# Looked-up expert rows on GpSimd and VectorE: another schedule of the row groups and another first write of the gates

## The chip, the cores and the metric

The kernel runs on one core of one Trainium2 chip. The metric is the device time of one execution in microseconds. Three runs of the kernel before gave 4428.84, 4426.54 and 4429.15 us (median 4428.84).

## The reference, cut to what matters

One layer: a mixing stage (latent attention beside an RWKV scan), a cross attention, and a product-key expert layer ("PEER"), each added to the residual; 1024 tokens of width 1024, all in f32. The change touches the last of them alone:

```python
s = einsum('bshpd,hpkd->bshpk', q, sub_keys)         # 8 heads, 2 halves, 128 keys each
v1, i1 = top_k(s[..., 0, :], 16); v2, i2 = top_k(s[..., 1, :], 16)
cv, ci = top_k((v1[..., :, None] + v2[..., None, :]).reshape(..., 256), 16)
expert = e1 * 128 + e2                               # one of 16384, e1 and e2 by ci
gate = softmax(cv)
u = expert_u[it]; pre = einsum('tkd,td->tk', u, xt)  # it: 8 x 16 experts of a token
act = gelu(pre) * gate
out = einsum('tk,tkd->td', act, expert_v[it])
```

## The kernel before, in words

The stage `peer_stage` treats the 8 tiles of 128 tokens in two ways.

**Dense tiles.** Tiles 0 to 5 meet every expert. A first phase of 128 blocks (one block is 128 experts) computes gelu(u x) on TensorE (`block_in`, L1979) and stores it in `hidden_d`. Meanwhile VectorE picks the 16 experts of each (head, tile) unit (`choose`, in six pieces), and GpSimd scatters the unit's 16 columns of gates into `gates_d`, one indirect DMA per column (L1960), adding to zeros that an earlier stage wrote. Then two output passes multiply hidden value and gate and sum over experts (`block_out`, L2070): pass 0 for tiles 0 to 3, 128 blocks; pass 1 for tiles 4 and 5, again 128 blocks. Each output block loads 512 KB of expert rows and two pieces of `hidden_d` and `gates_d`.

**Looked-up tiles.** Tiles 6 and 7 fetch their experts instead: 2 tiles x 8 heads x 16 = 256 look-ups, each an indirect DMA on GpSimd's queue (`look_up`, L1940) of one 8 KB row (u beside v) for each of 128 tokens, 1 MB. VectorE works on them in groups of two: `row_hidden` (L2348) takes the dot product with u, ScalarE the gelu, `row_sums` (L2360, L2363) adds gate x v to the sum. After `row_sums` the buffer is given back (`row_used`).

**What sets the order.** Every engine walks by hand-written slots: WT = 16 slots of the query projection, then slots 16 to 143 (the first phase), then 144 to 271 (pass 0) and 272 to 399 (pass 1). `unit_pieces` says in which slots a unit is chosen: one unit per slot up to slot 14, then one unit in three slots. `group_slot` says in which slot a group's dot products stand, `sums_at` in which its sums. The first EARLY_SLOTS look-ups use a ring of 8 buffers, all later ones a ring of 6 (`RING_IN`, `RING_OUT`): look-up p waits until row p - 8, or p - 6, was given back.

GpSimd's queue holds scatters and look-ups in one line. `rows_by` spreads EARLY_SLOTS look-ups evenly over the 384 scatters of dense units 7 to 30, and PASS_SLOTS over the 256 scatters of units 32 to 47; the rest follows behind the last scatter. The first look-up of the second ring waits for the end of the first phase. Pass 1 may load gates only when all scatters have landed. A waiting look-up holds up all scatters behind it.

Of the kernel before, what the change touches and what calls it, by code (L numbers as in the profile page):

```python
# [10 lines left out]
ALU = mybir.AluOpType  # L11
# [22 lines left out]
NK = 128  # L34
# [1617 lines left out]

DENSE = NT - 2
PASSES = ((0, 1, 2, 3), (4, 5))
EARLY_SLOTS, PASS_SLOTS = 148, 64
RING_IN, RING_OUT = 8, 6
TD = DENSE * P
HD = TD // 2
# [4 lines left out]
GROUP = 2  # L1663
HOME_ROWS = 4
WT = 2 * PH
FIRST_UNIT = 4


def unit_order():
# [6 lines left out]
def unit_pieces():  # L1676


    at, slot = {}, FIRST_UNIT
    for n in range(UNITS):  # L1680
# [9 lines left out]
def peer_stage(nc, consts, h, high, low, rstd, w_query, keys_d, expert_u, expert_uv, fin_row, scores_d, hidden_d, gates_d, h_d,  # L1690
# [10 lines left out]
    OUT = WT + NK  # L1701
    with Stage(nc, "peer") as st:
# [15 lines left out]
        idx, gates = st.sb("idx", [P, UNITS, TOPK], U32), st.sb("gates", [P, UNITS, TOPK])  # L1718
# [31 lines left out]
        added = [st.sem(f"added{i}") for i in range(4)]  # L1750
# [43 lines left out]
        def group_slot(g):  # L1794

            if g < EARLY_SLOTS // GROUP:
                return WT + 14 + (g * 29) // 20
            g -= EARLY_SLOTS // GROUP
            if g < PASS_SLOTS // GROUP:
                return OUT + 4 + (g * 17) // 5  # L1800
            return OUT + NK + 2 + 5 * (g - PASS_SLOTS // GROUP)

        groups = SLOTS // GROUP
        groups_at = {group_slot(g): g for g in range(groups)}
        gelu_at = {group_slot(g) + 2: g for g in range(groups)}
        lasts = (EARLY_SLOTS // GROUP - 1, groups - 1)
        sums_at = {group_slot(g) + 4 if g in lasts else group_slot(g + 1) + 2: g for g in range(groups)}
        assert len(groups_at) == len(gelu_at) == len(sums_at) == groups
        row_end = max(sums_at) + 1

# [18 lines left out]
        def _(sp):  # L1829
# [8 lines left out]
            def load_raw(b):  # L1838
                if b >= 3:
                    sp.wait_ge(u_low, b - 2)  # L1840
                sp.dma_start(raw[b % 3][:, :], w_query[b] if b < WT else expert_u[b - WT]).then_inc(raw_ready[b % 3], 16)
# [34 lines left out]
            for b in range(WT):  # L1876
                load_raw(b + 3)
                if b >= 2:
                    store_scores(b - 2)
                if b == FIRST_UNIT - 1:  # L1880
                    load_scores(0)
                    load_scores(1)
                next_scores(b)
# [37 lines left out]
        @block.gpsimd  # L1921
        def _(pool):
            def look_up(p):
                n, k = row_place(p)[1:]
                buffer, ready, use = rows(p)
                pool.wait_ge(idx_ready, n + 1)
                if p == 0:
                    pool.wait_ge(h_stored, 16)
                    pool.wait_ge(rows_full, 2 * SPARSE)
                    pool.wait_ge(scaled, 2 * KC)  # L1930
                    pool.wait_ge(s_mm, WT)
                    for i in range(2):
                        pool.wait_ge(w_stored[i], 16 * PH)
                if p < EARLY_SLOTS and p >= RING_IN:
                    pool.wait_ge(row_used, p - RING_IN + 1)
                if p == EARLY_SLOTS:
                    pool.wait_ge(mm_done, WT + NK)
                if p >= EARLY_SLOTS + RING_OUT:
                    pool.wait_ge(row_used, p - RING_OUT + 1)
                pool.indirect_dma_start(buffer[:, :], None, expert_uv,  # L1940
                                        bass.IndirectOffsetOnAxis(ap=idx[:, n, k:k + 1], axis=0)).then_inc(ready, 16)

            def add_squares():
                for m in range(KC // 2):
                    pool.wait_ge(sq_ready, 2 * m + 2)
                    if m >= 2:
                        pool.wait_ge(sq_summed, m - 1)
                    nc.gpsimd.tensor_tensor(sq_sum[:, m % 2, :], sq[:, 0, :], sq[:, 1, :], ALU.add).then_inc(sq_added, 1)

            nc.gpsimd.iota(iota_i[:, :], [[1, TOPK]], base=0, channel_multiplier=0).then_inc(iota_ready, 1)  # L1950
            nc.gpsimd.iota(tok_i[:, :], [[P, NT]], base=0, channel_multiplier=1).then_inc(iota_ready, 1)
            add_squares()
            turn = 0
            for i, n in enumerate(dense):
                head, tile = units[n]
                pool.wait_ge(idx_ready, n + 1)
                if scatters(head - 1, tile):
                    pool.wait_ge(added[tile % 4], scatters(head - 1, tile))
                for k in range(TOPK):
                    pool.indirect_dma_start(gates_flat, bass.IndirectOffsetOnAxis(ap=idx[:, n, k:k + 1], axis=0),  # L1960
                                            gates[:, n, k:k + 1], None, compute_op=ALU.add).then_inc(added[tile % 4], 16)
                    for p in range(turn, rows_by(i, k)):
                        look_up(p)
                    turn = max(turn, rows_by(i, k))
            for p in range(turn, SLOTS):
                look_up(p)
            for tile in range(4):
                pool.wait_ge(added[tile], scatters(PH - 1, tile + 4 if tile + 4 < DENSE else tile))
# [630 lines left out]
```

## Time and profile before

| | us |
|---|---|
| median of 3 runs | 4428.84 |
| profiled execution, its own time | 4427.99 |
| its span in the trace | 4426.4 |
| first phase, first block_in matmul to last | about 1891 to 3116 |
| pass 0, output blocks | about 3144 to 3930 |
| pass 1, to the last matmul | about 3938 to 4416 |

Times in the trace count from the start of the span. The share of an engine over the whole span says little here, since the three phases have different limits; the tables by stretch are to be read, and in them the busy time of each engine beside the stretch's length. GpSimd's busy time leaves out some 0.30 us ahead of each of its DMAs, which the profile calls issue; the two together are what one DMA costs that queue.

### The profile page before, as it was taken

To read this page: it belongs to the slowest core of one execution; us is meant where nothing else is said; L and a number is where in the kernel's file an instruction comes from. 1 tells how busy PE (TensorE), PEld (TensorE's weight loads), DVE (VectorE), ACT (ScalarE), POOL (GpSimd) and SP (SyncE) were. 2 spreads that over 40 slices of the span, in tenths; PEclk is the share of its full clock that TensorE was granted. 3 is DMA by queue.
4 is the path that set the end of the run, shared out by engine and by line. 5 is a ranking of instruction groups with operands and counts; after the bars stand their busy time and mean duration, and the time that the engine had idled before them with its cause. 6 is when DMAs were issued, how large, how long until landed. Compare 5 with 4: busy or idle time off the path is not lost.

```text
span 4426.4 us, 54973 instructions
## 1 busy us (share of the span) xinstructions
PE 3834.4 (87%) x19168; PEld 3258.1 (74%) x19168; DVE 2790.5 (63%) x5235; ACT 1263.5 (29%) x1846; POOL 2019.4 (46%) x1384
## 2 busy tenths in 40 slices
PE   7958788888888889999889888989789999988878
PEld 5834377787766567899889888889667777876666
DVE  5453367677313336847777777767798666557776
ACT  2113323332102212233232222222333222233334
POOL 1023132424000001888878888887567888301110
PEclk9979889898889999999999999999999999998899
DMA  2249200000221023548788878876778899869886
GB/s 100 95 158 400 107 17 8 17 8 8 72 90 38 0 71 105 93 92 265 235 254 244 243 235 244 249 246 185 249 235 269 271 281 290 283 215 307 306 308 230
DMA packets 376334, 788.59 MB, mean 178 GB/s; under 512 B 137104, under 2 KB 211856, under 8 KB 342288
## 3 DMA queue, kind: packets, MB, share of 16 engines
q1 hardware_dynamic: 210320, 451.28, 30.4%
q0 software_dynamic: 165888, 336.01, 26.0%
q8 instruction: 33, 0.54, 0.1%
q14 instruction: 93, 0.76, 0.0%
HBM read 643.09 MB, written 144.05 MB: 178 GB/s over the span
## 4 chain that ended last, share of the span: by engine, by line
PE 14%; DMA 13%; DVE 12%; POOL 9%; issue 8%; DVEq 3%; ACT 2%; SPq 1%; POOLq 0%; ACTq 0%
POOL gates_d L1960 7%; PE peer_ps L2070 5%; PE peer_ps L1979 5%; DVE peer_acc L2363 4%; PE peer_ps L1993 4%; DMA late_in<-gates_d 3%; DMA peer_rows<-in_expert_uv,peer_idx 3%; DMA late_rows<-in_expert_uv,peer_idx 3%; DMA rows<-in_expert_uv,peer_idx 2%; DMA peer_gat<-gates_d 1%; DVEq L2278 1%; DVEq L2362 1%; POOL peer_rows L1940 1%; DVE late_in L2370 1%; DVE peer_rows L2348 1%
## 5 line engine op out<-in xcount | busy, mean ns | idle before, releaser
L1960 POOL DMA_INDIRECT gates_d<-peer_gates,peer_idx x768 | 1353.3, 1762 | 320.9 <-issue 219.7
L1979 PE MATMUL peer_ps<-high,peer_uh 128*128 128x384 f32 x2048 | 540.4, 345 | 116.3 <-DVE peer_ul L2265 105.5
L1979 PE MATMUL peer_ps<-low,peer_uh 128*128 128x384 f32 x2048 | 533.5, 342 | 0.0
L1979 PE MATMUL peer_ps<-high,peer_ul 128*128 128x384 f32 x2048 | 531.7, 341 | 0.0
L1979 PEld LDWEIGHTS peer_ps<-high,peer_uh 128*128 128x128 f32 x2048 | 377.8, 194 | 133.1 <-issue 107.4
L2070 PE MATMUL peer_ps<-peer_vh,peer_ah 128*128 128x512 f32 x1028 | 339.5, 413 | 103.7 <-DVE peer_al L2382 103.6
L1940 POOL DMA_INDIRECT late_rows<-in_expert_uv,peer_idx x108 | 140.1, 1297 | 562.9 <-DVE peer_acc L2363 497.0
L2116 ACT ACTIVATE peer_uh<-peer_raw 128x1024 fp32r<-128x1024 f32 x144 | 152.4, 1058 | 813.5 <-PE peer_ps L1979 698.9
L1979 PEld LDWEIGHTS peer_ps<-low,peer_uh 128*128 128x128 f32 x2048 | 382.0, 194 | 0.0
L1979 PEld LDWEIGHTS peer_ps<-high,peer_ul 128*128 128x128 f32 x2048 | 381.2, 193 | 0.0
L2070 PE MATMUL peer_ps<-peer_vh,peer_al 128*128 128x512 f32 x1028 | 331.5, 405 | 0.0
L2070 PE MATMUL peer_ps<-peer_vl,peer_ah 128*128 128x512 f32 x1028 | 329.5, 403 | 0.0
L2070 PEld LDWEIGHTS peer_ps<-peer_vh,peer_ah 128*128 128x128 f32 x1028 | 199.8, 199 | 162.8 <-DVE peer_al L2382 121.6
L2265 DVE TENSOR_TENSOR peer_ul<-peer_raw,peer_uh 128x1024 fp32r<-128x1024 f32 x144 | 177.2, 1231 | 96.4 <-ACT peer_uh L2116 87.3
L2070 PEld LDWEIGHTS peer_ps<-peer_vh,peer_al 128*128 128x128 f32 x1028 | 202.9, 197 | 45.4
L2070 PEld LDWEIGHTS peer_ps<-peer_vl,peer_ah 128*128 128x128 f32 x1028 | 201.7, 196 | 44.9
L2348 DVE CUSTOM_DVE_ANT_0 late_rows<-late_rows,peer_xrow 128x1024 f32<-128x1024 f32 x108 | 129.5, 1221 | 138.5 <-DMA late_rows<-in_expert_uv,peer_idx 138.5
L2070 PE MATMUL peer_ps<-peer_uh,peer_ah 128*128 128x512 f32 x508 | 169.1, 415 | 53.5 <-DVE peer_al L2382 53.5
L2164 ACT ACTIVATE peer_ah<-late_in 128x512 fp32r<-128x512 f32 (+1 forms) x170 | 88.2, 519 | 285.5 <-DVE late_in L2370 268.9
L2070 PE MATMUL peer_ps<-peer_uh,peer_al 128*128 128x512 f32 x508 | 166.0, 409 | 0.0
L2070 PE MATMUL peer_ps<-peer_ul,peer_ah 128*128 128x512 f32 x508 | 165.7, 408 | 0.0
L2070 PEld LDWEIGHTS peer_ps<-peer_uh,peer_ah 128*128 128x128 f32 x508 | 98.6, 198 | 83.7 <-DVE peer_al L2382 61.7
(437 smaller groups left out, 7858.0 us busy)
## 6 DMA issues: line engine op xcount, KB each, us to landing
late_in<-in_expert_uv SPq DMA_DIRECT2D x170, 512.0 KB
gates_d<-mla_zeros POOLq DMA_DIRECT2D x128, 512.0 KB
peer_raw<-in_expert_u SPq DMA_DIRECT2D x128, 512.0 KB
hidden_d<-peer_hid SPq DMA_DIRECT2D x128, 384.0 KB
peer_val<-in_expert_uv SPq DMA_DIRECT2D x86, 512.0 KB
late_in<-hidden_d SPq DMA_DIRECT2D x85, 256.0 KB
late_in<-gates_d SPq DMA_DIRECT2D x85, 256.0 KB
gates_d<-peer_gates,peer_idx POOLq DMA_INDIRECT x768
```

The costliest lines, as they stand in the source:

```text
L1940: pool.indirect_dma_start(buffer[:, :], None, expert_uv, bass.IndirectOffsetOnAxis(ap=idx[:, n, k:k + 1], axis=0)).then_inc(ready, 16)
L1960: pool.indirect_dma_start(gates_flat, bass.IndirectOffsetOnAxis(ap=idx[:, n, k:k + 1], axis=0), gates[:, n, k:k + 1], None, compute_op=ALU ...
L1979: last = nc.tensor.matmul(ps[i][:, a, 0:HD], w[:, cols], x[:, kc, a * HD:(a + 1) * HD], start=(kc == 0 and w is uh[i % 2] and x is high), ...
L1993: last = nc.tensor.matmul(ps[i][:, a, :], w[:, cols], x[:, kc, a * HALF:(a + 1) * HALF], start=(kc == 0 and w is uh[i] and x is high), sto ...
L2070: last = nc.tensor.matmul(ps[i][:, a, :], x[:, i * P:(i + 1) * P], w[:, a * HALF:(a + 1) * HALF], start=(first_block and x is ah[r] and w ...
L2116: nc.scalar.activation(uh[b % 2][:, :], raw[b % 3][:, :], ACT.Copy).then_inc(u_high, 1)
L2164: nc.scalar.activation(ah[q % RING][:, 0:n], act_in[q % 3][:, 0:n], ACT.Copy).then_inc(a_high, 1)
L2265: nc.vector.tensor_tensor(ul[b % 2][:, :], raw[b % 3][:, :], uh[b % 2][:, :].bitcast(F32), ALU.subtract).then_inc(u_low, 1)
L2278: dve.drain()
L2348: nc.vector.tensor_tensor_reduce(out=buffer[:, 0:D], in0=buffer[:, 0:D], in1=xrow[row_place(p)[0]][:, :], scale=1.0, scalar=0.0, op0=ALU.m ...
L2362: dve.drain()
L2363: nc.vector.scalar_tensor_tensor(out=acc[tile][:, :], in0=rows(p)[0][:, D:2 * D], scalar=pre[:, p:p + 1], in1=acc[tile][:, :], op0=ALU.mul ...
```

## The change

Five edits in one file:

- EARLY_SLOTS and PASS_SLOTS go from 148, 64 (44 left) to 144, 72 (40 left): four look-ups fewer in the first phase, eight more in pass 0, four fewer behind it.
- Early groups stand 4 slots later (WT + 18 instead of WT + 14, the same 29/20 slots between them). Groups of pass 0 stand every 3 slots from OUT + 7, instead of every 3.4 from OUT + 4. Those of pass 1 keep their slots, but there are two groups fewer.
- The sums of all groups from the last early one on follow 3 slots behind the dot products. Before, they stood 2 slots behind the next group's dot products.
- FIRST_UNIT is 3, not 4: the first unit is chosen one slot sooner, 12 instead of 11 units fit in ahead of the first phase, and all later units move three slots forward. The load of the first scores stays where it was.
- For head 0 the scatter writes the gates (`bypass`) and does not add them.

```diff
-EARLY_SLOTS, PASS_SLOTS = 148, 64
+EARLY_SLOTS, PASS_SLOTS = 144, 72
-FIRST_UNIT = 4
+FIRST_UNIT = 3
             if g < EARLY_SLOTS // GROUP:
-                return WT + 14 + (g * 29) // 20
+                return WT + 18 + (g * 29) // 20
             g -= EARLY_SLOTS // GROUP
-            if g < PASS_SLOTS // GROUP:
-                return OUT + 4 + (g * 17) // 5
-            return OUT + NK + 2 + 5 * (g - PASS_SLOTS // GROUP)
+            return OUT + 7 + 3 * g if g < PASS_SLOTS // GROUP else OUT + NK + 2 + 5 * (g - PASS_SLOTS // GROUP)
-        lasts = (EARLY_SLOTS // GROUP - 1, groups - 1)
-        sums_at = {group_slot(g) + 4 if g in lasts else group_slot(g + 1) + 2: g for g in range(groups)}
+        sums_at = {group_slot(g) + 3 if g >= EARLY_SLOTS // GROUP - 1 else group_slot(g + 1) + 2: g for g in range(groups)}
-                if b == FIRST_UNIT - 1:
+                if b == FIRST_UNIT:
-                                            gates[:, n, k:k + 1], None, compute_op=ALU.add).then_inc(added[tile % 4], 16)
+                                            gates[:, n, k:k + 1], None, compute_op=ALU.add if head else ALU.bypass
+                                            ).then_inc(added[tile % 4], 16)
```

GpSimd's queue where pass 0 begins. `gates_d<-peer_gates` is a scatter, `late_rows` a look-up into the second ring; the first `late_rows` waits for the end of the first phase. Before:

```order
L1940 DMA rows<-in_expert_uv,peer_idx 128x2048
L1960 DMA gates_d<-peer_gates,peer_idx 16777216x1 x20
L1940 DMA late_rows<-in_expert_uv,peer_idx 128x2048
L1960 DMA gates_d<-peer_gates,peer_idx 16777216x1 x4
L1940 DMA late_rows<-in_expert_uv,peer_idx 128x2048
L1960 DMA gates_d<-peer_gates,peer_idx 16777216x1 x4
L1940 DMA late_rows<-in_expert_uv,peer_idx 128x2048
```

and now:

```order
L1937 DMA peer_rows<-in_expert_uv,peer_idx 128x2048
L1957 DMA gates_d<-peer_gates,peer_idx 16777216x1 x20
L1937 DMA late_rows<-in_expert_uv,peer_idx 128x2048
L1957 DMA gates_d<-peer_gates,peer_idx 16777216x1 x4
L1937 DMA late_rows<-in_expert_uv,peer_idx 128x2048
L1957 DMA gates_d<-peer_gates,peer_idx 16777216x1 x3
L1937 DMA late_rows<-in_expert_uv,peer_idx 128x2048
```

Four scatters stood between two look-ups; now there are three and four in turn, mostly.

VectorE's order in the later part of pass 0, where no more units are chosen. A block is the three rows that end in `peer_al`; the four ISA rows are a group's dot products, and `peer_pre` with `peer_acc` are the sums that give two buffers back. Before:

```order
L2360 TENSOR_TENSOR peer_pre<-peer_pre,peer_gates 128x2
L2363 SCALAR_TENSOR_TENSOR peer_acc<-late_rows,peer_pre,peer_acc 128x1024 x2
L2370 TENSOR_TENSOR late_in<-late_in 128x512
L2378 TENSOR_TENSOR peer_vl<-late_in,peer_vh 128x1024
L2382 TENSOR_TENSOR peer_al<-late_in,peer_ah 128x512
L2348 ISA late_rows,peer_pre<-late_rows,peer_xrow 128x1024
L2348 ISA peer_pre 128x1
L2348 ISA late_rows,peer_pre<-late_rows,peer_xrow 128x1024
L2348 ISA peer_pre 128x1
```

and now:

```order
L2346 ISA late_rows,peer_pre<-late_rows,peer_xrow 128x1024
L2346 ISA peer_pre 128x1
L2346 ISA late_rows,peer_pre<-late_rows,peer_xrow 128x1024
L2346 ISA peer_pre 128x1
L2358 TENSOR_TENSOR peer_pre<-peer_pre,peer_gates 128x2
L2361 SCALAR_TENSOR_TENSOR peer_acc<-late_rows,peer_pre,peer_acc 128x1024 x2
L2368 TENSOR_TENSOR late_in<-late_in 128x512
L2376 TENSOR_TENSOR peer_ul<-late_in,peer_uh 128x1024
L2380 TENSOR_TENSOR peer_al<-late_in,peer_ah 128x512
```

The sums of a group now stand right behind the dot products of the next group, three blocks after its own; before, they stood two blocks behind the next group's, five or six after its own.

## Rows read from the trace of the kernel before

**Rows 1.** Busy time by stretch, all engines; (x) counts instructions
```profile
core 0: us, PE busy (x) PEld busy (x) DVE busy (x) ACT busy (x) POOL busy (x), PEclk, DMA share, GB/s
1766.00:1995.00 229.00, 220.67 (x1198) 202.12 (x1197) 152.91 (x464) 63.08 (x82) 194.25 (x115) 0.99 0.49 95
2050.00:3048.00 998.00, 888.81 (x4867) 874.49 (x4866) 759.79 (x1835) 289.76 (x407) 813.76 (x501) 0.94 0.81 244
3117.00:3395.00 278.00, 223.46 (x897) 174.23 (x896) 234.41 (x587) 90.56 (x127) 186.16 (x111) 0.93 0.82 255
3395.00:3804.00 409.00, 392.46 (x1672) 318.25 (x1672) 266.86 (x352) 115.28 (x161) 347.10 (x204) 0.98 0.92 283
3804.00:3930.00 126.00, 125.18 (x579) 103.37 (x578) 60.32 (x78) 36.15 (x50) 8.33 (x6) 1.00 0.64 217
3938.00:4324.00 386.00, 309.62 (x1162) 243.45 (x1161) 281.87 (x432) 145.31 (x225) 51.67 (x40) 0.87 0.90 307
4332.00:4411.00 79.00, 71.73 (x294) 56.59 (x295) 59.51 (x90) 38.21 (x58) 0.00 (x0) 0.96 0.75 243
```

**Rows 2.** GpSimd's groups, 2050 to 3048: count, busy, mean ns, idle before and its releasers
```profile
L1960 POOL DMA_INDIRECT gates_d<-peer_gates,peer_idx x361 | 635.8, 1761 | 110.0 <-issue 101.2 <-DVE peer_acc L2363 8.8
L1940 POOL DMA_INDIRECT peer_rows<-in_expert_uv,peer_idx x68 | 90.3, 1328 | 35.1 <-issue 20.5 <-DVE peer_acc L2363 13.5 <-DVE peer_idx L2333 0.6
L1940 POOL DMA_INDIRECT rows<-in_expert_uv,peer_idx x72 | 90.0, 1250 | 39.4 <-DVE peer_acc L2363 20.5 <-issue 17.1 <-DVE peer_idx L2335 1.2
```

**Rows 3.** Timeline of GpSimd: start, duration, instruction, idle before it
```profile
1766.04 1.68 POOL L1960 DMA_INDIRECT gates_d<-peer_gates,peer_idx  x1 [87.21 <-DVE peer_idx L2335]
...
1995.66 1.02 POOL L1940 DMA_INDIRECT rows<-in_expert_uv,peer_idx  x1 [0.30 <-issue]
...
2050.67 1.00 POOL L1940 DMA_INDIRECT rows<-in_expert_uv,peer_idx  x1 [0.30 <-issue]
...
3047.48 0.99 POOL L1940 DMA_INDIRECT rows<-in_expert_uv,peer_idx  x1 [0.30 <-DVE peer_idx L2335]
...
3116.89 1.00 POOL L1940 DMA_INDIRECT late_rows<-in_expert_uv,peer_idx  x1 [28.09 <-PE peer_ps L1979]
...
3197.81 1.43 POOL L1940 DMA_INDIRECT late_rows<-in_expert_uv,peer_idx  x1 [24.94 <-DVE peer_acc L2363]
...
3804.29 2.39 POOL L1960 DMA_INDIRECT gates_d<-peer_gates,peer_idx  x1 [0.30 <-issue]
```

**Rows 4.** Timeline of VectorE, the first group: dot product, then sums
```profile
2019.96 1.21 DVE L2348 CUSTOM_DVE_ANT_0 rows<-rows,peer_xrow 128x1024 f32<-128x1024 f32 x1
...
2045.14 2.67 DVE L2363 SCALAR_TENSOR_TENSOR peer_acc<-rows,peer_pre,peer_acc 128x1024 f32<-128x1024 f32 x2
```

**Rows 5.** Chain of work that ended last: start, us, what
```profile
1721.26 10.91 PE peer_ps L1993 x48
1732.17 1.78 PE peer_ps L2017 x16
...
1912.65 116.76 PE peer_ps L1979 x672
...
3375.44 22.27 PE peer_ps L2070 x96
```

**Rows 6.** Who waited for whom, 2000 to 3000: us in total, times, longest
```profile
DVE peer_rows L2348 <- DMA peer_rows<-in_expert_uv,peer_idx: 106.6, 30, 7.7
DVE rows L2348 <- DMA rows<-in_expert_uv,peer_idx: 67.2, 20, 7.8
```

**Rows 7.** GpSimd's groups, 3117 to 3806
```profile
L1960 POOL DMA_INDIRECT gates_d<-peer_gates,peer_idx x252 | 453.3, 1799 | 76.8 <-issue 71.6 <-DVE peer_acc L2363 4.9 <-DVE peer_idx L2335 0.3
L1940 POOL DMA_INDIRECT late_rows<-in_expert_uv,peer_idx x63 | 82.5, 1309 | 105.3 <-DVE peer_acc L2363 61.0 <-PE peer_ps L1979 28.1 <-issue 16.2
```

**Rows 8.** VectorE's product of hidden value and gate, one a block, 4332 to 4411
```profile
L2370 DVE TENSOR_TENSOR late_in<-late_in x16: 418/421/428, 4333.8 to 4404.2; 128x256 f32<-128x256 f32 x16
L2370 DVE TENSOR_TENSOR peer_act_in<-peer_act_in,peer_gat x8: 418/420/426, 4340.5 to 4406.7; 128x256 f32<-128x256 f32 x8
```

**Rows 9.** Who GpSimd waited for, 3930 to 4330
```profile
POOL late_rows L1940 <- DVE peer_acc L2363: 436.0, 20, 110.1
```

**Rows 10.** SyncE's load of the first scores, and VectorE's slot 3
```profile
1713.31 0.80 SPq L1836 DMA_DIRECT2D peer_sc<-scores_d  x2
...
1719.51 1.23 DVE L2272 TENSOR_TENSOR peer_q<-peer_ps,rstd 128x1024 f32<-128x1024 f32 x1 [7.69 <-PE peer_ps L1993]
```

**Rows 11.** All scatters of the span: min/median/max ns
```profile
L1960 POOL DMA_INDIRECT gates_d<-peer_gates,peer_idx x768: 1539/1571/2629, 1766.0 to 3804.3; - x192
```

**Rows 12.** DMA issues of the output passes on SyncE's queue: count, KB each
```profile
late_in<-in_expert_uv SPq DMA_DIRECT2D x170, 512.0 KB
...
late_in<-hidden_d SPq DMA_DIRECT2D x85, 256.0 KB
late_in<-gates_d SPq DMA_DIRECT2D x85, 256.0 KB
```

## The prediction, written before the changed kernel ran

> **What bounds the kernel now.** I read the busy time by stretch first, then GpSimd's groups, its timeline, the chain of waits and the waits.
>
> First phase. From 2050 to 3048 TensorE is busy for 889 of 998 us, and VectorE for 760 [rows 1]. GpSimd is busy for 814 us, and its 501 DMAs have 0.30 us of issue ahead of each, 150 us: 964 of 998. What is left, 34 us, are waits for a row buffer [rows 2]. So GpSimd's queue bounds it: a scatter costs 1.76 + 0.30 = 2.06 us, a look-up 1.29 + 0.30 = 1.59. VectorE's waits for looked-up rows, 106.6 + 67.2 us [rows 6], are how TensorE feels this queue. Up to 2029 no row holds anything: 672 matmuls of 48 a block take 116.76 us, 8.34 us a block [rows 5].
>
> Pass 0. From 3117 to 3395 VectorE is the fullest, 234 of 278 us, since it still chooses units. From 3395 to 3804 GpSimd is: 347 busy + 204 x 0.30 = 408 of 409 us [rows 1]. Once its last scatter is out at 3804 [rows 3], TensorE is busy for 125 of 126 us and the DMA share falls from 0.92 to 0.64 [rows 1].
>
> Pass 1. To 4324 the DMA engines are at 0.90 and 307 GB/s, behind it at 0.75 and 243 GB/s [rows 1]. GpSimd waits 20 times, 436 us in all, for buffers [rows 9], and is no bound; the look-ups' traffic is.
>
> **First phase, part by part.** *Groups four slots later.* Eight look-ups fill the ring by 2050.67, when the ninth starts at once [rows 3], because the first sums began at 2045.14, in slot 17 of the phase [rows 4]. Now the first sums stand in slot 21. Blocks run at 8.34 us there, so they begin at 2045.1 + 4 x 8.34 = 2078.5, the first buffer is back at 2079.9, and the ninth look-up starts at about 2081: 30.4 us later. Behind it in the queue wait 360 scatters and the other look-ups, and all of the phase waits for them. FIRST_UNIT = 3 lets the queue start 12.7 us sooner (a product of 10.91 us and its scores of 1.78 are a slot there [rows 5]), and a scatter written faster would too; both only lengthen this wait, so they are worth 0 here. *Four look-ups fewer:* 4 x 1.59 = -6.4. *Waits for the ring:* per group the queue now has 384/72 = 5.33 scatters, not 384/74 = 5.19, 0.3 us more, so it catches up with VectorE less often. The 34 us can shrink by 0 to 34; I take -6, near the low end, as the ring and the spacing of the groups are the same. *Last group:* slot 18 + 102 = 120 of the phase instead of 14 + 105 = 119, so one block less is left behind it: -8.3. Sum: 30.4 - 6.4 - 6 - 8.3 = **+10 us**, bounds -18 and +24.
>
> The earlier unit itself adds nothing: the first scores are loaded at 1713.31 and VectorE opens slot 3 at 1719.51 after 7.69 us of idle time [rows 10]. If its cover were gone it would cost one unit's choice, at most one slot of 12.7 us.
>
> **Pass 0.** The queue restarts when the first phase ends, as before. *Eight look-ups more:* 8 x (1.31 + 0.30) = +12.9 [rows 7]. *Ring:* waits for a buffer are 61 us here, 24.94 of them ahead of the seventh look-up [rows 3, 7]. It is now reached some 6 us sooner (21 scatters ahead of it, not 24) and its buffer comes in slot 10 instead of 9, some 6 us later: +12. Then come groups every 3 slots with 17.9 us of queue each (7.11 x 2.10 + 2 x 1.61) against some 7 us a slot while VectorE is full: 3 us of wait for each of some six groups, where the eight other waits before were 36 us: about -8 to -18 by how many remain. I take +4 for both; bounds -36 (all but the first wait go) and +12. *Last group* in slot 7 + 105 = 112, not 109: 3 blocks x 5.57 us (96 matmuls take 22.27 us, a block has 24 [rows 5]) fewer behind it, 16.7 us, of which I count -14, since its own rows are worked late. *More traffic* beside it: +2, bounds 0 and +22 (below). *Units three slots sooner* take one unit's work from VectorE's full stretch; it is in the ring's estimate. *Written gates:* 32 of pass 0's scatters are of head 0. If such a scatter cost what a look-up does, they would save 32 x 0.49 = 16 us, most of it ahead of the ring's first wait; if they cost the same, 0. The shortest scatter there is takes 1.54 us [rows 11]; I take 0. Sum: 12.9 + 4 - 14 + 2 = **+5 us**.
>
> On the write: from 1766 to 1995 the DMA engines show a share of 0.49 at only 95 GB/s while 115 scatters of 128 elements run [rows 1], so small elements cost them time out of proportion to their bytes. The Trainium skill, "DMA: Bandwidth & Descriptors", Specifications, says that transfers under 512 B are done as read-modify-write in any case. By it a written 4-byte gate saves the DMA engines nothing; without it the share could fall. No row shows a written scatter, and the sum is the same either way.
>
> **Pass 1.** Before, a pair of look-ups goes out every five blocks (386 us with 20 pairs: 19.6 us a pair, 3.92 a block) [rows 1, 9]. Behind them 24 products stand between 4333.8 and 4406.7, 23 steps of 3.17 us [rows 8]. Now 34 look-ups are left for this stretch, not 40: four move away and two more fit in early, as buffers come back sooner. The last pair goes out 14 blocks sooner (before at slot 227, two behind group 126's; now at 213). 14 x (3.92 - 3.17) = **-11 us**, bounds -17 (all of the freed blocks at 2.78, half of 5.57) and -7.
>
> **Sum.** +10 + 5 - 11 = +4 us on the profiled execution's 4427.99 (span 4426.4 and 1.6 around it), so 4432 us. That execution lies 0.85 us below the median of 4428.84.
>
> **The rivals.** *Forecast: a near draw with the first phase lost and pass 1 won*, 4432. For it: every stretch has a row that names its limit, and the terms are of one size with opposite signs. Against: four terms of 10 us each from estimates. Its own range is 4419 to 4446.
>
> *Slower: the DMA engines take over pass 0.* From 3395 on they are at a share of 0.92 [rows 1]. A block there moves 1 MB (1.05 million bytes) [rows 12] and its part of a group's 2.1 MB: before 1.05 + 2.1/3.4 = 1.67 MB, now 1.05 + 2.1/3 = 1.75 MB, 5% more, in 7.11/3 instead of 8/3.4 scatters. If 0.92 is the ceiling, 82 blocks of 6 us get 4.4% longer: +22 instead of +2, so 4452 us. It decides from the point where a look-up takes over 10 us to land. For it: pass 1 stays at 0.90 while everything waits for loads. Against: pass 1 moves 307 GB/s at that share, pass 0 283, and GpSimd alone explains pass 0's pace.
>
> *Faster: buffers that come back sooner free the queue.* Of the ring's 61 us in pass 0 half the 36 behind the first wait goes, with no later wait in its place: -18 instead of +4, so 4410 us; with written gates that save something it goes below. For it: sums 3 slots behind the dot products, not 5.4, and one unit less in VectorE's full stretch. Against: until 3395 VectorE is at 234 of 278 us, and a queue that stops waiting there gains only what VectorE can use.
>
> *The change doesn't act:* four blocks of lead are made up at the first wait for the ring and the phases keep their lengths: 4428.
>
> **How the numbers follow.** Chances: forecast 0.44, DMA ceiling 0.26, freed queue 0.25, no action 0.05. A difference under 0.2%, 9 us, can't be told from none in this kernel. Faster (below 4420): 0.22 of the third case and 0.05 of the first, 0.27. Slower (above 4438): 0.24 of the second and 0.12 of the first, 0.36. Within: 0.37. The range takes in both other cases: 4404 to 4455.
>
> **What would show it.** The first phase's last matmul at 3126 instead of 3116; a wait of some 40 us ahead of GpSimd's ninth look-up, which starts at 2081; its last early look-up at about 3065. In pass 0 the first wait for the ring near 37 us, the last scatter some 28 us later than 3804, blocks of 6.0 us between; pass 0's last matmul at about 3945. In pass 1 look-ups that end 14 blocks sooner, and 11 us less from there to the end. Wrong it is if the ninth look-up isn't late, or if it is and the first phase still ends by 3116 (then GpSimd had slack that I didn't see); if scatters of head 0 are visibly shorter than 1.54 us; or if the DMA share in pass 0 passes 0.94 with blocks over 6.2 us.

## The result, and the profile after

The changed kernel took 4473.55 us (median of 4 runs: 4468.55, 4484.27, 4473.16, 4473.93), the kernel before 4428.99 in the same measurement. The ratio is 1.0108 [1.009, 1.0127]: 1.1% slower. I had forecast 4432 and a range up to 4455.

The table cuts both profiled executions at TensorE's own products, so that one stage's loss doesn't shift the next one's figure. The query projection runs from its first matmul to its last, and the first phase ends where its last matmul begins. Each output pass ends with matmuls against the identity (`peer_ps<-ident,rest`): pass 0 is cut at the first of these, pass 1 at the last. The later executions of the same changed kernel stand beside it, since they are needed below.

| us | before | after, recorded | after again (b1) | after again (c1) | scatters all added (a1) |
|---|---|---|---|---|---|
| query projection | 214.1 | 263.3 | 214.1 | 264.3 | 214.2 |
| first phase | 1244.2 | 1241.7 | 1252.2 | 1254.0 | 1246.0 |
| pass 0 | 799.9 | 814.0 | 812.6 | 808.5 | 812.7 |
| pass 1 | 500.4 | 480.3 | 481.7 | 480.9 | 480.1 |

The span grew by 4467.0 - 4426.4 = 40.6 us, and +49.2 - 2.5 + 14.1 - 20.1 = +40.7. The three stages that I priced at +4 came out at -8.5. The whole loss stands in the query projection, a stage for which I had no term. Each column is one execution; the same program's first phase alone differs by up to 15 us from one to the next (1239.1 in d1, 1254.0 in c1), so a few microseconds in it mean little.

The matmuls by line in the trace of after; each row ends with the first and last start, which is where the table comes from (the stage's last one starts within a microsecond of these):

```profile
L1991 PE MATMUL peer_ps<-high,peer_uh x256: 388/389/793, 1657.3 to 1919.7; 128*128 128x512 f32 x128
...
L1977 PE MATMUL peer_ps<-high,peer_uh x2048: 331/334/690, 1926.2 to 3161.6; 128*128 128x384 f32 x187
```

Before, the same two lines begin at 1657.4 and 1877.1. The median matmul is not longer (389 and 334 ns in both). Over the projection TensorE is busy for 209.9 of 214.1 us before and for 224.0 of 263.3 after: some 35 of the 49 us are idle time between matmuls, and the other 14 are longer matmuls where the clock was low (the mean over the projection is 0.90, before 0.99). The table by stretch of after, with the columns of [rows 1]; the stretch 1766 to 1995 answers to its first row:

```profile
1766.00:1780.00 14.00, 5.86 (x19) 3.58 (x17) 5.91 (x29) 0.00 (x0) 10.64 (x12) 0.74 0.18 48
1780.00:1800.00 20.00, 4.30 (x16) 3.83 (x16) 2.41 (x5) 0.00 (x0) 10.81 (x12) 0.50 0.01 0
1800.00:1900.00 100.00, 88.72 (x399) 72.89 (x399) 66.62 (x235) 15.80 (x28) 49.44 (x44) 0.88 0.29 73
1766.00:1995.00 229.00, 186.76 (x923) 161.88 (x922) 127.89 (x386) 47.29 (x64) 151.31 (x114) 0.87 0.34 78
3444.00:3853.00 409.00, 383.06 (x1619) 308.74 (x1618) 268.46 (x356) 111.63 (x157) 347.76 (x202) 0.97 0.91 285
```

From 1780 to 1800 TensorE works 4.30 of 20 us, VectorE 2.41, ScalarE nothing, and the DMA engines move nothing (share 0.01). GpSimd alone goes on. The granted clock, 1.00 up to 1766, falls to 0.50, which is 1.2 GHz, behind idle time. The last row is the later part of pass 0, where my rival on the DMA engines was to show; it stands 49 us later than the row of [rows 1], as the pass begins 47 us later. The share is 0.91 at 285 GB/s (before 0.92 at 283), and a block takes 6.06 us (1619 matmuls, 24 a block; before 1672 and 5.87 us), under the 6.2 us and the share of 0.94 that I had named for that rival. GpSimd's queue is full as before: 347.76 + 202 x 0.30 = 408.4 of 409 us.

What TensorE's idle time is put down to, from its timeline:

```profile
1785.16 0.37 PE L2015 MATMUL peer_ps<-peer_keys,peer_q 128*128 128x128 f32 x1 [3.12 <-issue]
1787.96 0.37 PE L2015 MATMUL peer_ps<-peer_keys,peer_q 128*128 128x128 f32 x1 [2.43 <-issue]
1790.06 0.37 PE L2015 MATMUL peer_ps<-peer_keys,peer_q 128*128 128x128 f32 x1 [1.73 <-issue]
1792.86 0.37 PE L2015 MATMUL peer_ps<-peer_keys,peer_q 128*128 128x128 f32 x1 [2.43 <-issue]
```

Issue is time for which no semaphore and no queue in the trace answers. The starts are 2.80, 2.10 and 2.80 us apart, multiples of 0.70 us. The chain that ended last in after, to be laid beside [rows 5]:

```profile
1782.04 3.12 issue
1785.53 2.43 issue
...
1872.01 10.91 PE peer_ps L1991 x48
1882.92 1.78 PE peer_ps L2015 x16
...
1960.42 199.93 PE peer_ps L1977 x1152
```

With the gaps gone a slot is 10.91 + 1.78 us again, as before. The undisturbed stretch of the first phase holds 24 blocks (1152 matmuls of 48) at 8.33 us and not 14; the groups stand later.

GpSimd's timeline, where the first scatter has moved ahead and become short:

```profile
1753.41 1.06 POOL L1957 DMA_INDIRECT gates_d<-peer_gates,peer_idx  x1 [74.63 <-DVE peer_idx L2333]
1754.78 1.00 POOL L1957 DMA_INDIRECT gates_d<-peer_gates,peer_idx  x1 [0.30 <-issue]
1756.09 0.96 POOL L1957 DMA_INDIRECT gates_d<-peer_gates,peer_idx  x1 [0.30 <-issue]
...
1806.70 0.96 POOL L1957 DMA_INDIRECT gates_d<-peer_gates,peer_idx  x1 [12.53 <-DVE peer_idx L2333]
```

and all its scatters, min/median/max ns:

```profile
L1957 POOL DMA_INDIRECT gates_d<-peer_gates,peer_idx x768: 954/1578/2636, 1753.4 to 3879.6; - x192
```

A written scatter takes 0.96 us; of the added ones none took under 1.54 [rows 11]. The first starts 12.6 us before the first scatter of [rows 3]. The gaps open some 16 us after it, a dozen written scatters on, and close within a few microseconds after a batch of them is out. GpSimd's own next unit then comes late (12.53 us of waiting), since VectorE stood still too. The 64 early ones go out in three batches, whose last scatters start at 1793, 1826 and 1849; TensorE's gaps put down to issue lie at 1769 to 1798, 1822 to 1829 and 1845 to 1852, and nowhere else in the projection. The 32 written scatters where pass 0 begins cost that pass nothing that shows: 814.0 us here and 808.5 in c1, 812.6 in b1, which had no such gaps.

The ninth look-up, on which my largest term rests, and the ring's waits in pass 0. Waits of GpSimd in after, 1995 to 3110 and then 3170 to 3860 (columns as in [rows 6]):

```profile
POOL rows L1937 <- DVE peer_acc L2361: 81.9, 8, 68.4
...
POOL late_rows L1937 <- DVE peer_acc L2361: 92.1, 7, 59.4
```

The longest of the first row, 68.4 us, is the ninth look-up's; before there was none [rows 3]. The packets of the page changed as well, first before, then after:

```profile
DMA packets 376334, 788.59 MB, mean 178 GB/s; under 512 B 137104, under 2 KB 211856, under 8 KB 342288
```

```profile
DMA packets 365582, 788.59 MB, mean 177 GB/s; under 512 B 126352, under 2 KB 201104, under 8 KB 331536
```

That is 10752 fewer for 96 written scatters, 112 each: where an added one shows 144 packets of 4 bytes, a written one shows 32, 16 of 4 bytes and 16 of 32. The DMA engines spend far less time on them. From 1766 to 1835 the queue of scatters takes 20.5% of the 16 engines' time before, with 37 added scatters, and 1.8% in b1, with 55 written ones:

```profile
q0 software_dynamic: 5127, 0.02, 20.5%
...
q0 software_dynamic: 1696, 0.03, 1.8%
```

### The profile page after: what moved, and what is told of

Its sections match the earlier page's. It is cut to its first block, busy times and chain, and to the rows that moved or that the text cites. A ratio compares the mean times of both kernels' runs of the same rounds, so it can differ in the third digit from the quotient of the medians.

```text
span 4467.0 us, 54971 instructions
## 1 busy us (share of the span) xinstructions
PE 3847.2 (86%) x19168; PEld 3265.7 (73%) x19168; DVE 2789.5 (62%) x5235; ACT 1261.7 (28%) x1844; POOL 1946.2 (44%) x1384
## 4 chain that ended last, share of the span: by engine, by line
PE 15%; POOL 12%; DMA 12%; DVE 10%; issue 9%; DVEq 2%; ACT 1%; SPq 1%; POOLq 0%; ACTq 0%
POOL gates_d L1957 10%; PE peer_ps L1977 6%; PE peer_ps L2068 4%; PE peer_ps L1991 4%; DMA late_rows<-in_expert_uv,peer_idx 3%; DVE peer_acc L2361 3%; DMA peer_rows<-in_expert_uv,peer_idx 3%; DMA peer_gat<-gates_d 2%; DMA late_in<-gates_d 2%; DVEq L2276 1%; DMA rows<-in_expert_uv,peer_idx 1%; POOL peer_rows L1937 1%; POOL rows L1937 1%; DVEq L2360 1%; DVE late_rows L2346 1%
## 5 line engine op out<-in xcount | busy, mean ns | idle before, releaser
L1957 POOL DMA_INDIRECT gates_d<-peer_gates,peer_idx x768 | 1285.4, 1674 | 377.3 <-issue 220.4
L2068 PE MATMUL peer_ps<-peer_uh,peer_ah 128*128 128x512 f32 x508 | 178.2, 434 | 89.8 <-DVE peer_al L2380 75.8
```

Source lines behind the costliest of these rows:

```text
L2068: last = nc.tensor.matmul(ps[i][:, a, :], x[:, i * P:(i + 1) * P], w[:, a * HALF:(a + 1) * HALF], start=(first_block and x is ah[r] and w ...
```

## The experiments

One theory at the start was that the written gates bring the gaps; its rival, that FIRST_UNIT = 3 does, by scatters that start earlier beside the query projection. All medians below are of runs beside the kernel before on the same chip.

**First measurement** (before 4422.33).

a1_added, the changed kernel with

```diff
-compute_op=ALU.add if head else ALU.bypass
+compute_op=ALU.add
```

> The changed kernel with the gates of head 0 added to the zeros, as before, and all else as changed. Theory W (the written scatters hold up every engine while more than about a dozen of them follow each other): the query stage, 49 us longer in the changed kernel, is back at 214 us (1657 to 1871), the output passes' start is some 10 us quicker, and the time is 4473.5 - 49 - 10 = 4414 us, between 4405 and 4424. Theory U (the unit chosen one slot sooner holds up VectorE and with it TensorE in the query stage): the 49 us stay, and the time is 4465 or more.

Measured 4423.31, ratio 0.9998 [0.9984, 1.0013], query projection 214.2 us. The long stage is gone, with the early scatters still there (the first one at 1757.5). Its waits, at the ninth look-up (1995 to 3110) and for the ring of pass 0 (3110 to 3834, the last scatter):

```profile
POOL rows L1937 <- DVE peer_acc L2361: 55.5, 10, 45.2
...
POOL late_rows L1937 <- DVE peer_acc L2361: 69.0, 7, 40.7
```

a2_before_written, the kernel before with `ALU.add if head else ALU.bypass`.

> The kernel before with the gates of head 0 written and nothing else changed. Theory W: the query stage is 40 to 50 us longer, TensorE shows gaps there that nothing it waits for explains, and the time is 4429 + 49 + 10 = 4488 us, between 4470 and 4495. Theory U: the time stays at 4429, or is a little lower, since a written scatter takes GpSimd 0.96 us and not 1.55.

Measured 4428.37, 1.0005 [0.9991, 1.002], stage 214.1. The write alone, on the kernel before, did not bring it.

a3_before_first3, the kernel before with the earlier unit:

```diff
-FIRST_UNIT = 4
+FIRST_UNIT = 3
-                if b == FIRST_UNIT - 1:
+                if b == FIRST_UNIT:
```

> The kernel before with the first unit chosen one slot sooner and nothing else changed. Theory W: no harm in the query stage (214 us, as before); the ninth look-up can start only with the first buffer given back, so at most 3 us are won in the first phase, and one unit less in VectorE's full stretch wins some 5 to 8 us in pass 0: 4420 us, between 4415 and 4429. Theory U: the query stage takes up to 49 us more, 4470 us.

Measured 4409.88, 0.9977 [0.9963, 0.9991]: the first phase is 13.0 us shorter (1231.2) and pass 0 6.6 (793.3). This edit by itself makes the kernel faster, and by more than I had expected: the ninth look-up starts 3.4 us sooner, as forecast (175.8 us after the last query product, before 179.2), and no run says where in the first phase the other 10 us come from.

a4_paced, the changed kernel with a wait behind each written scatter until it has landed:

```diff
+                    if not head:
+                        pool.wait_ge(added[tile % 4], 16 * (k + 1) + scatters(head - 1, tile))
```

> The changed kernel, but GpSimd waits after each written scatter of head 0 until it has landed. If it is the number of written scatters in flight at once that holds up the engines: the query stage is back at 214 us and the time is that of the kernel with added gates, about 4414 us, or up to 15 us more for GpSimd's waits in pass 0. If each written scatter does its harm by itself, the 49 us stay: 4473 us.

Measured 4457.43, 1.008 [1.0053, 1.0107]. The stage is 214.1, but the waits cost GpSimd more than they could save: 67 of them up to 3150, and the first phase became 1268.4 us.

```profile
POOL gates_d L1957 <- DMA gates_d<-peer_gates,peer_idx: 128.9, 67, 5.8
```

What followed from these four looked settled: writes together with the earlier unit. It was not.

**Second measurement** (before 4423.27).

b1_after_again is the changed kernel, unaltered.

> The changed kernel itself, beside the others on one chip. The kernel before with written gates showed no stall in its query stage and was 0.05% slower; with gates added the changed kernel was level (0.9998). Theory I (written scatters and the unit one slot sooner do harm only together): the query stage is 263 us long again and the time is 1.0% above the kernel before. Theory C (the stall belonged to the executions of the first measurement, and is no property of the program): the stage takes 214 us and the time is within 0.3% of the kernel before.

Measured 4428.87, 1.0011 [0.9996, 1.0027], and the stage is 214.1 us. The same program, 45 us faster than in the recorded measurement. By stretch, to be laid beside after's:

```profile
1766.00:1780.00 14.00, 14.00 (x71) 11.86 (x71) 12.23 (x47) 2.26 (x4) 10.95 (x11) 1.00 0.31 87
1780.00:1800.00 20.00, 20.00 (x106) 17.13 (x105) 17.73 (x62) 4.52 (x8) 15.13 (x17) 1.00 0.38 103
```

TensorE is busy for every microsecond, while the same short scatters go out at the same time (the first at 1753.25).

b2_before_first3_written is a3 with head 0 written as well.

> The kernel before with the first unit one slot sooner and the gates of head 0 written; shares and slots of the look-ups as before. Theory I: about 1.0% slower than the kernel before, with a query stage near 260 us, since both parts of the pair are there. Theory C: as with added gates, 0.2% faster than the kernel before, or up to 10 us above that for pass 0's written scatters.

Measured 4419.52, 0.9989 [0.9974, 1.0004], stage 214.1.

b3_after_first4 is the changed kernel with FIRST_UNIT = 4 and the load of the first scores where it was.

> The changed kernel with the first unit in slot 4 as before; gates written, shares and slots changed. Theory I: no stall in the query stage (214 us), and the time of the changed kernel with added gates plus one unit's work in pass 0: 0 to 0.4% above the kernel before. Theory L (the stall needs written scatters and something of the changed look-up schedule): the stall stays, 1.0% slower.

Measured 4440.58, 1.0033 [1.0016, 1.0049]. Against b1 the first phase is the same (1249.5 and 1252.2), pass 0 is 7.6 us longer (820.2) and the time 11.7 us.

b4_written_pass0 writes only the gates of tiles 4 and 5, which are scattered in pass 0:

```diff
-compute_op=ALU.add if head else ALU.bypass
+compute_op=ALU.add if head or tile < 4 else ALU.bypass
```

> The changed kernel with the gates of head 0 added for tiles 0 to 3 and written only for tiles 4 and 5, 32 scatters where pass 0 begins. The query stage takes 214 us by every theory. If written scatters also hold up the start of pass 0, its length stays at 814 us or more, as in the changed kernel, and the time is 0.2 to 0.4% above the kernel before; if not, it is level with the one where all gates are added (0.9998).

Measured 4426.97, 0.9997 [0.998, 1.0014], pass 0 809.9 us against a1's 812.7.

**Third measurement** (before 4420.6), on the same chip as the second.

c1_after_third is the changed kernel again.

> The changed kernel a third time, in another measurement. Its first measurement had a query stage of 263 us in the trace and a time 1.1% above the kernel before; its second had 214 us and 0.1%. If the long stage comes and goes with the program's load or its chip, a third measurement shows one of the two again, in all its executions: 1.0 to 1.1% or 0.0 to 0.3%. If the first was a single event, it shows the second.

Measured 4479.87 (four runs from 4462.89 to 4485.22), 1.0122 [1.0091, 1.0154]. The long stage is back, 264.3 us, on the chip that had not shown it before.

```profile
1785.00:1800.00 15.00, 3.40 (x7) 1.72 (x7) 2.99 (x12) 0.00 (x0) 11.40 (x12) 0.50 0.02 1
```

c2_before_later, the kernel before with its early groups four slots later:

```diff
-                return WT + 14 + (g * 29) // 20
+                return WT + 18 + (g * 29) // 20
```

> The kernel before with the early groups four slots later and nothing else changed. Theory R (the ring's first wait pushes GpSimd's queue back and the later place of the last group pays for it): GpSimd waits some 28 to 33 us ahead of the ninth look-up, four blocks of 8.34 us fewer stand behind the last group, and the first phase keeps its length within 5 us of 1244; the time is level with the kernel before (within 0.2%). Theory S (four blocks of lead hide the landing of the rows): the first phase gets 15 us or more shorter and the time falls by 0.4%.

Measured 4426.36, 1.0012 [0.9996, 1.0029]. This is my largest single term by itself. GpSimd's ninth look-up waits, up to 2110:

```profile
  DVE peer_acc L2363: 31.6, 1
```

Counted from the last query product it starts 28.3 us later than before (2071.85 - 1864.4 against 2050.67 - 1871.5; forecast 30.4), and the first phase grows by 0.9 us (1245.1). The wait is there in full; four blocks fewer are left behind the last group, 4 x 8.34 = 33 us, and they give it back. In the same stretch as c1's row TensorE is busy for 15.00 of 15:

```profile
1785.00:1800.00 15.00, 15.00 (x76) 12.69 (x75) 13.30 (x50) 2.26 (x4) 12.57 (x9) 1.00 0.53 90
```

c3_early_kept, the changed kernel with the gates added and the early part as before:

```diff
-EARLY_SLOTS, PASS_SLOTS = 144, 72
+EARLY_SLOTS, PASS_SLOTS = 148, 72
-                return WT + 18 + (g * 29) // 20
+                return WT + 14 + (g * 29) // 20
-compute_op=ALU.add if head else ALU.bypass
+compute_op=ALU.add
```

> The changed kernel with gates added, and the first phase's 148 look-ups and slots as before; 72 look-ups in pass 0 and 36 behind. By the parts as measured: a first phase like that of the kernel before with the unit one slot sooner (1231 us in place of 1246), pass 0 as in the changed kernel (813), and pass 1 shorter by four look-ups more, 461 in place of 480: some 34 us under the changed kernel with added gates in the trace, 0.6 to 0.8% faster than the kernel before.

Measured 4408.1, 0.997 [0.9955, 0.9985]: faster than both kernels. First phase 1236.5, pass 0 808.7, pass 1 474.7 us (I had expected 461 there).

c4_all_written writes the gates of every head (`compute_op=ALU.bypass`).

> The changed kernel with the gates of all heads written and none added, so that where two heads chose one expert for a token only the last gate counts. Every scatter should then take GpSimd 0.96 us and not 1.76. If GpSimd's queue bounds the first phase and pass 0, the first phase falls from 1250 us to between 1090 and 1160, what TensorE (128 blocks of 8.34 us) and VectorE need, and pass 0 from 813 to between 730 and 780. If the landing of rows or the DMA engines bound them, they shrink by less than 40 us each. If many written scatters in a row stall all engines, as in the first measurement's query stage, gaps without a releaser appear on TensorE throughout.

One run, 4473.94; the query projection is 309.6 us, the longest of all. In the first phase GpSimd now waits instead of bounding (1995 to 3215):

```profile
POOL rows L1937 <- DVE peer_acc L2361: 164.6, 15, 74.0
POOL peer_rows L1937 <- DVE peer_acc L2361: 158.4, 19, 20.1
```

Yet the phase takes 1245.1 us (a1 1246.0); I had expected 1090 to 1160. TensorE's only waits from 2080 to 3200 are of the kind that the long stage has:

```profile
PE peer_ps L1977 <- issue: 72.9, 134, 2.0
PE peer_ps L1977 <- DVE peer_ul L2263: 0.3, 1, 0.3
```

In a1 the second of these was 100.7 us and the first absent, so the gaps took the place of the wait for VectorE. Pass 0 fell to 770.7 us, 42 less than a1's, and in its later part TensorE is never idle:

```profile
3490.00:3866.00 376.00, 376.00 (x1642) 307.60 (x1641) 277.49 (x365) 113.02 (x160) 264.49 (x209) 1.00 0.92 320
```

So the scatters' cost bounds that part in the other kernels. Written ones relieve GpSimd and the DMA engines at once, and which of the two counts more this run can't separate. Whether the first phase would be short without the gaps, no run tells.

**Fourth measurement** (before 4422.46).

d1_after_fourth is the changed kernel again.

> The changed kernel a fourth time. So far the measurement it was in decided: query stage 263 and 264 us and 1.1 to 1.2% slower in two measurements, 214 us and level in one. This run says which of the two this measurement is, and the three beside it are read against that.

Measured 4434.82, 1.0032 [1.0017, 1.0047]; stage 214.1. The profiled execution was the fastest of the eight (4413.12), the others took 4424.2 to 4439.16.

d2_before_written2 is a2 again.

> The kernel before with the gates of head 0 written, a second time; the first was in a measurement where no query stage was long. If the long stage needs only written scatters and the right measurement, and the changed kernel shows it here, this kernel shows it too: a stage of some 260 us and 40 to 55 us more time. If it also needs the changed schedule, the stage is 214 us beside a long one of the changed kernel.

Measured 4426.39, 1.0007 [0.9985, 1.0028]; stage 214.1.

d3_paced_by_four waits at every fourth written scatter only (`if not head and k % 4 == 3`).

> The changed kernel, with GpSimd waiting after every fourth written scatter of head 0 until it has landed. In the long stages the gaps on TensorE begin some 16 us, a dozen written scatters, after the first. If what piles up behind written scatters holds the engines up, four at a time are too few: a query stage of 214 us even where the changed kernel has 263, and a time level with the kernel before. If every written scatter does its part, the stage stays long.

Measured 4421.49, 0.9985 [0.9967, 1.0003]. The pacing is nearly free: 16 waits up to 3150.

```profile
POOL gates_d L1957 <- DMA gates_d<-peer_gates,peer_idx: 24.5, 16, 2.8
```

d4_gates_moved puts an unused tensor ahead of the gates in memory:

```diff
+        nc.dram_tensor("unused_d", (9, P, T + 96), F32)
```

> The changed kernel with an unused tensor of 5.2 MB ahead of gates_d in device memory, so that the written gates lie elsewhere. If the place of the gates in memory decides over the long stage, this kernel and the changed one can differ in one measurement. If the state of the chip or of the process decides, they are alike.

Measured 4426.5, 1.0018 [1.0005, 1.003]; stage 214.1. Since d1 had no long stage either, it says nothing on placement.

**Fifth measurement** (before 4417.36).

e1_after_fifth, the changed kernel.

> The changed kernel a fifth time. Two of four measurements had the long query stage (4470 us and more), two had not (4429 and 4435). Either is possible here; it says how the kernel beside it is to be read, and whether all executions of one measurement again agree.

Measured 4426.36, 1.0013 [0.9987, 1.004]; no long stage.

e2_paced_again is d3 again.

> The changed kernel with a wait after every fourth written scatter of head 0, again. Beside a changed kernel with the long stage it decides whether the number of written scatters in flight matters: 214 us and a level time if so, 263 us and 1.1% if not. Beside a changed kernel without it, it shows again what the pacing costs or saves by itself: it was 0.15% faster than the kernel before, and the changed kernel 0.3% slower, in one measurement.

Measured 4421.63, 1.0001 [0.9976, 1.0025]. No paced kernel ever ran beside a long one, so whether pacing prevents the gaps stays open.

**What is shown and what is open.** Shown in the traces of after, c1 and c4: the lost time lies in gaps beside the written scatters. In c1, too, the three early batches end at 1802, 1835 and 1858, and the gaps of the projection lie at 1776 to 1806, 1829 to 1838 and 1853 to 1862 alone. c4, with more written scatters there, has the longer stage, 310 us, and has gaps in the first phase as well.

Strongly suggested: without a run of written scatters beside the query projection there are no such gaps. In the third measurement the two kernels that write early had the long stage and the two that add (c2, c3) had 214 us. But c2 and c3 also keep part of the old schedule, and no kernel that differs from the changed one by the adding alone (a1, b4) ran in a measurement with a long stage. Of all programs, none of those without early written scatters showed it, and of the runs with them only three did (after, c1, c4).

Written scatters are not enough either: a2, d2 and b2 wrote early and were not long, in measurements where no other kernel was long, and b1, d1 and e1 are the very program that was long. A trace shows one execution; that the others of a measurement agreed with it is read from their times. What differs from one measurement to the next I didn't find in the traces. It isn't the chip alone, since one chip had both. Where a program's memory lies when it is loaded would fit, but that was only argued.

A small remainder is open too. Without the long stage the changed kernel was at 1.0011, 1.0032 and 1.0013, and the same with all gates added (a1) at 0.9998; d1's interval [1.0017, 1.0047] and a1's [0.9984, 1.0013] don't meet, and beside d1 the paced kernel d3 was at 0.9985. So written scatters may cost up to 0.3% without a long stage; e1 and e2 (1.0013 and 1.0001) can't tell the two apart.

## Why the prediction was wrong, point by point

**The step that failed** is the pricing of the written gates. I wrote "I take 0", bounded by a gain of 16 us alone, and of the queue's early part that "a scatter written faster would too; both only lengthen this wait, so they are worth 0 here". I looked only at what the scatter costs GpSimd. That no row showed a written scatter called for a bound on the other side too, a harm to whoever runs beside it. It measured +49.2 us in the recorded run and +50.2 in c1, and 0 in b1, d1 and e1. Where it is absent my sum stood within 0.3%: a1 0.9998, b1 1.0011, d1 1.0032, e1 1.0013, against 4432 / 4428.84 = 1.0007. In part that is luck, since pass 0 and pass 1 both missed, with opposite signs. The stage terms that follow are read from the traces, and there "measured" is the range over the profiled executions of the changed kernel.

As to the gain: the scatter is in fact 0.6 us shorter (0.96 against 1.55), beyond my bound, which had it as long as a look-up, 1.29, and under the 1.54 that I had named as a sign of being wrong. Still nothing came of it. a2 and d2 against before are 1.0005 and 1.0007, b2 against a3 0.9989 and 0.9977: 96 x 0.6 = 58 us of GpSimd's time, most of it ahead of waits that it only lengthens (68.4 us in b1 where a1 has 45.2, and 56.4 where it has 40.7 in pass 0). That half of the step held. From the Trainium skill, "DMA: Bandwidth & Descriptors", Specifications, by which transfers under 512 B are done as read-modify-write, I had drawn that a written gate saves the DMA engines nothing. The trace does not agree: the share of the scatters' queue fell from 20.5% to 1.8%. It brought no time in that stretch, in which TensorE is busy for 69.00 of 69 us before and in b1.

**First phase, +10 forecast.** Measured -2.5 in after, +8.0 in b1, +9.8 in c1, -5.1 in d1 and +1.0 in e1, and +1.8 in a1: single executions that differ by more than the term. The late look-up came out as forecast, within 3 us: in b1 it starts 207.3 us after the last query product, before 179.2, so 28.1 us later for 30.4, and in c2 28.3. The giving back behind the last group also held. The waits for the ring were not the 34 us that I had left over from the sum but 42.8 us, by the releasers in [rows 2] (8.8 + 13.5 + 20.5); GpSimd's issue time there is 138.8 us and not 150. That widens the bound of the term of -6 and leaves the term. That FIRST_UNIT = 3 is worth 0 here held in the changed kernel (b3 against b1). Without the four slots' delay it is worth 13.0 us (a3), so the two edits together threw away a gain that one alone had. I had the sentence that says so, and didn't follow it to the better kernel. c3, with the early part as before, keeps most of it (1236.5 against 1244.2).

**Pass 0, +5 forecast, +8.6 to +14.1 measured**, +12.8 in a1, which has no written gates and answers to my terms. From the phase's start to the last scatter: before 3804.3 - 3115.7 = 688.6, a1 3832.5 - 3121.5 = 711.0, so +22.4 where my terms gave 12.9 + 4 + 2 = 18.9. The ring's term was too small: all its waits up to the last scatter are 69.0 us against 61.0, +8.0 for +4. Its shape was right, one wait of 40.7 us (forecast 37) and then six of 3.2 to 5.1 us (forecast 3), where before eight of 0.3 to 8.2 us made up the 36. Behind the last scatter: 111.3 and 101.7, -9.6 where I took -14. These two misses, of some 4 us each, are the whole difference.

**Pass 1, -11 forecast, -15.5 to -20.1 measured** (a1 -20.3), mostly outside its bound of -17. The number of blocks was right and their price was off. GpSimd's look-ups of this pass in b1, and VectorE's products behind the last of them, one a block, first before and then b1:

```profile
L1937 POOL DMA_INDIRECT late_rows<-in_expert_uv,peer_idx x34: 969/1292/1421, 3960.8 to 4283.4; - x34
...
L2370 DVE TENSOR_TENSOR late_in<-late_in x18: 418/421/428, 4321.4 to 4404.2; 128x256 f32<-128x256 f32 x18
L2370 DVE TENSOR_TENSOR peer_act_in<-peer_act_in,peer_gat x9: 418/420/426, 4331.2 to 4406.7; 128x256 f32<-128x256 f32 x9
...
L2368 DVE TENSOR_TENSOR late_in<-late_in x27: 417/419/426, 4284.1 to 4405.5; 128x256 f32<-128x256 f32 x27
L2368 DVE TENSOR_TENSOR peer_act_in<-peer_act_in,peer_gat x14: 416/422/426, 4288.1 to 4408.8; 128x256 f32<-128x256 f32 x14
```

Before, 27 products stand behind the last look-up; now 41 do, 14 more, as I had said. Up to the last look-up the pass takes 405.2 us before (3915.6 to 4320.8) and in after 347.2 (3976.3 to 4323.5), 58.0 less; behind it 95.2 and 133.1, 37.9 more. So 14 blocks left a pace of 4.14 us for one of 2.71, and 14 x 1.43 = 20. Of the two prices the later one was further off: my 3.17 was the mean of the last 24 blocks before [rows 8], in which the last groups' own work still ran. The last 13 steps before take 2.83 us each, and so do the last 23 in b1.

**The rivals.** *DMA ceiling:* its signs didn't appear. The share is 0.91 with blocks of 6.06 us in after, looked-up rows land in 8.1 us (median of b1, 3403 to 3812; I had named 10), and pass 0 grew by at most 14.1 us where this rival had 25. *Freed queue:* not borne out; the ring's waits grew (61.0 to 69.0 us in a1). *No action:* pass 0 grew and pass 1 shrank in every execution, so the phases did not keep their lengths; the time of a kernel without the long stage can't tell this rival from my forecast. That the change is slower was forecast with a chance of 0.36, but by another mechanism.

## What to carry to other kernels

Where an edit brings a form of instruction that the trace doesn't show, bound what it may do to the engines beside it, not only its own time. Price edits singly as well as together: one of this change's edits was worth 0.23% alone (a3), and the whole gave it away in front of a ring whose groups stand later. And run an unaltered program again in another measurement before explaining a loss of a per cent: four experiments agreed here on a cause, written gates together with the earlier unit, that the fifth, the same kernel once more, took back.

## What the runs showed of the hardware that I had not expected

- TensorE, VectorE, ScalarE and the DMA engines can nearly stop together for tens of microseconds, with gaps put down to issue in steps of some 0.70 us, while GpSimd has written 4-byte scatters out (after: TensorE 4.30 us busy in 20, 0 GB/s). With the same program it was there in 2 of 5 measurements, each time with the times of all executions alike within 0.5%.
- An indirect scatter of 128 four-byte elements costs GpSimd 0.96 us where it writes and 1.55 where it adds, and 32 packets instead of 144. 37 added ones took 20.5% of the DMA engines' time in 69 us, 55 written ones 1.8%.
- Without added scatters pass 0 takes 770.7 us against 812.7 (c4 and a1, one execution each), and TensorE, busy for 376.00 of 376 us, bounds its later part.
